# A hybrid decoder block on one Trainium2 core: seven products in the last MLP pass of a group, and the next rows normalised and split one pass earlier

## The reference

```
u = rmsnorm(x) @ w_in                     # 1024 x 3608, split by column
h_m = mLSTM over chunks of 64 (4 heads);  h_g = gated linear attention (4 heads)
x = x + concat(h_m, h_g) @ w_out
x = x + softmax(rmsnorm(x) @ wq_x @ K^T / 16) @ V @ wo_x      # K, V from mem, 4 heads
x = x + square(relu(rmsnorm(x) @ w1)) @ w2                    # 1024 -> 4096 -> 1024
out = rmsnorm(x)
```

## Time and profile before

| | |
|---|---|
| median of three runs | 2837.98 us (2837.52 to 2838.74) |
| the profiled execution | 2838.17 us, its span 2836.6 us |
| instructions | 44515 |
| granted TensorE clock, mean | 0.999 of full speed |
| DMA | 375.50 MB, 132 GB/s on average |
| TensorE / VectorE / ScalarE / GpSimd busy | 99% / 63% / 52% / 33% of the span |

### The profile page before, as it was taken

The page is one execution under the profiler, slowest core; times in us unless marked ns, Lnnn a source line. Parts: engine busy times, 40 slices in busy tenths (PEclk is TensorE's granted clock), DMA queues, the critical chain, the costliest instruction groups (busy, mean ns, idle before and its releaser), DMA issues.

```text
span 2836.6 us, 44515 instructions
## 1 busy us (share of the span) xinstructions
PE 2814.4 (99%) x15148; PEld 2341.6 (83%) x15148; DVE 1778.3 (63%) x2969; ACT 1467.3 (52%) x3006; POOL 924.4 (33%) x1214
## 2 busy tenths in 40 slices
PE   8999999999999999999999999999999999999998
PEld 8888888888888888888888878888888888888887
DVE  6476774666576755556767675466557675545665
ACT  6554444555455444554645544455545544455553
POOL 5264553444135400232326320044322540023430
PEclk9999999999999999999999999999999999999999
DMA  6732575544542222354454222254454223234442
GB/s 218 246 105 68 176 265 176 190 151 133 136 165 82 76 89 90 111 171 142 146 148 146 68 83 90 90 186 147 131 146 164 82 72 92 91 98 147 149 149 82
DMA packets 178823, 375.50 MB, mean 132 GB/s; under 512 B 13808, under 2 KB 13952, under 8 KB 178592
## 3 DMA queue, kind: packets, MB, share of 16 engines
q1 hardware_dynamic: 155216, 300.45, 34.3%
q0 software_dynamic: 20704, 67.33, 7.2%
q10 hardware_dynamic: 2672, 4.76, 0.5%
HBM read 332.60 MB, written 29.39 MB: 128 GB/s over the span
## 4 chain that ended last, share of the span: by engine, by line
PE 95%; DVE 2%; issue 1%; ACT 1%; DMA 0%; DVEq 0%; ACTq 0%
PE bank L1948 47%; PE work L1948 21%; PE bank L2314 14%; PE work L2314 2%; PE work L1962 1%; PE bank L2352 1%; PE work L2063 1%; PE bank L2032 1%; PE work L2101 1%; PE bank L1962 1%; PE work L2123 1%; DVE w_lo L1389 1%; PE work L2010 1%; DVE tok L1575 1%; PE work L2212 1%
## 5 line engine op out<-in xcount | busy, mean ns | idle before, releaser
L872 ACT ACTIVATE w_hi<-raw 128x512 fp32r<-128x512 f32 x1120 | 701.1, 630 | 1034.2 <-PE bank L1948 539.5
L1389 DVE TENSOR_TENSOR w_lo<-raw,w_hi 128x512 fp32r<-128x512 f32 x708 | 515.4, 732 | 837.9 <-ACT w_hi L872 836.5
L1387 DVE SCALAR_TENSOR_TENSOR w_lo<-raw,w_hi 128x512 fp32r<-128x512 f32 x412 | 368.7, 916 | 78.2 <-ACT w_hi L872 77.2
L1948 PE MATMUL bank<-act_hi,w_hi 128*128 128x512 f32 x848 | 333.3, 393 | 0.0
L1948 PE MATMUL bank<-act_lo,w_hi 128*128 128x512 f32 x848 | 330.2, 389 | 0.0
L1948 PE MATMUL bank<-act_hi,w_lo 128*128 128x512 f32 x848 | 330.2, 389 | 0.0
L725 POOL TENSOR_TENSOR hr<-qk 128x256 f32<-128x256 f32 x48 | 35.3, 736 | 784.2 <-ACT qk L1262 784.2
L1948 PE MATMUL bank<-w_hi,act_hi 128*128 128x512 f32 x640 | 255.2, 399 | 0.0
L1948 PE MATMUL bank<-w_lo,act_hi 128*128 128x512 f32 x640 | 249.6, 390 | 0.0
L1948 PE MATMUL bank<-w_hi,act_lo 128*128 128x512 f32 x640 | 249.5, 390 | 0.0
L2314 PE MATMUL bank<-w_hi,h_hi 128*128 128x512 f32 x576 | 224.5, 390 | 0.3
(11 more groups left out here) (391 smaller groups left out, 6075.5 us busy)
## 6 DMA issues: line engine op xcount, KB each, us to landing
raw<-in_w_dram SPq DMA_DIRECT2D x232, 512.0 KB, 3.8
raw<-in_w_in_dram SPq DMA_DIRECT2D x112, 512.0 KB, 3.6
raw<-sums_dram SPq DMA_DIRECT2D x96, 512.0 KB, 3.7
raw<-in_w_out_dram SPq DMA_DIRECT2D x32, 512.0 KB, 3.8
raw<-kq_dram SPq DMA_DIRECT2D x32, 512.0 KB, 3.7
raw<-vo_dram SPq DMA_DIRECT2D x32, 512.0 KB, 3.7
xres<-in_x_dram POOLq DMA_DIRECT2D x16, 512.0 KB, 6.5
early_rows<-in_w_dram POOLq DMA_DIRECT2D x6, 1024.0 KB, 8.9
```

The costliest lines, as they stand in the source:

```text
L872: nc.scalar.activation(w_hi[:, slot, :], raw[:, pair_slot, slot % 2, :], ACT.Copy).then_inc(slab_hi, 1)
L1387: ins = stt(out=w_lo[:, slot, :], in0=src, scalar=1.0, in1=hi, op0=ALU.mult, op1=ALU.subtract)
L1389: ins = tt(w_lo[:, slot, :], src, hi, ALU.subtract)
L1948: ins = mm(dst, left, right, start=(kt == 0 and j == 0), stop=(kt == KT - 1 and j == 2))
```

## The change

The last pass of the first three groups becomes a split pass too; the last group keeps `mlp_pass`. Four more weight sums are made (16 in all): eight through `early_rows`, six through `tok`, of which four wait for the probabilities, and two after `hidden_sums(0)`. The input and output projections get operand buffers of their own, `x_hi` and `x_lo`, which lie over `x_blocks` and `x_turned`; the mixer's smaller buffers now lie over `act_hi` and `act_lo`. The next rows are loaded in pass 1 and their squares, scaling and moves are in pass 2 (`NEXT_PASS`), between GpSimd's differences and S1/S2; the transposes and splits are in the last pass's first half. In the output projection VectorE makes the low parts of tiles 4 and 5 before the split at slab 58 (`FIRST_TURN` - 1). The ring of pairs becomes regular, so its table goes.

```diff
-GROUP_SLABS = MLP_AT[LAST] + 4 * KT
+GROUP_SLABS = MLP_AT[LAST] + PASS_SLABS
-GROUP_PRODS = 2 * PRODUCTS * LAST
+GROUP_PRODS = 2 * PRODUCTS * HB
+PRO_PRODS = 2
+FIRST_TURN = min(TURN_MIX)
-NEXT_SQUARES, NEXT_SCALES, NEXT_TURNS = 0, 5, 20
+NEXT_PASS, NEXT_SQUARES, NEXT_SCALES = HB - 2, 0, 5
+NEXT_TURNS = {1: (0, 1), 2: (2, 3), 3: (4, 5), 4: (6, 7)}
+NEXT_SPLITS = {5: (0, 1), 6: (2, 3), 12: (4, 5), 13: (6, 7)}
-N_SUMS = LAST * HALF
-EARLY_SUMS = 6
+N_SUMS = HB * HALF
+EARLY_SUMS, BEFORE_SUMS = 8, 14
...
+        def free_no(g, hb, q, tile):
+
+            return GROUP_PRODS * g + (PRO_PRODS + 2 * PRODUCTS * hb + 2 * q + tile + 1)
+
+        def sums_done(eng, n):
+
+            eng.wait_ge(sums_stored[n % 4], 16 * (n // 4 + 1))
...
-                def hidden_sums(hb):
+                def hidden_sums(hb, between=None):
...
                         nc.gpsimd.tensor_tensor(diff[:, kt, :], quarter(0, 0, kt), quarter(0, 1, kt),
                                                 ALU.subtract).then_inc(diff_ready, 1)
+                    if between is not None:
+                        between()
                     pool.wait_ge(operand_lo_dve, per_pass(g, N_DVE_LOW, hb, HALF))
...
                     for n in range(EARLY_SUMS):
                         weight_sums(n)
-                        if n in (2, 3):
-                            pool.wait_ge(sums_stored[n - 2], 16)
+                        if 2 <= n < 6:
+                            sums_done(pool, n - 2)
                             load_quarters(n + 2)
                     pool.wait_ge(norm_ss, PRO_ROWS + 16 * g + NCH)
                     load_quarters(EARLY_SUMS)
                     load_quarters(EARLY_SUMS + 1)
-                    for n in range(EARLY_SUMS, N_SUMS):
+                    for n in range(EARLY_SUMS, BEFORE_SUMS):
+                        if n == EARLY_SUMS + 2:
+                            pool.wait_ge(pr_ready, 8 * g + 8)
+                        if n < EARLY_SUMS + 4:
+                            sums_done(pool, n - 4)
                         weight_sums(n)
-                        if n + 2 < N_SUMS:
-                            pool.wait_ge(sums_stored[n], 16)
-                            load_quarters(n + 2)
+                        sums_done(pool, n)
+                        load_quarters(n + 2)
+
+                def next_rows():
+
+                    if first:
+                        for n in (N_SUMS - 2, N_SUMS - 1):
+                            sums_done(pool, n)
+                    if not final:
+                        for i in range(NCH):
+                            pool.dma_start(tok[:, i, :], A["x"][bass.ds((g + 1) * GROUP + i * P, P), :])\
+                                .then_inc(next_in, 16)
+
+                def next_blocks():
+
+                    pool.wait_ge(tok_ready, PRO_ROWS + 8 * g + NCH)
+                    stand_alone(pool)
+                    for n in range(16):
+                        move_blocks(n)
+
                 hidden_sums(0)
...
                 if first:
-                    for n in (N_SUMS - 2, N_SUMS - 1):
-                        pool.wait_ge(sums_stored[n], 16)
...
-                hidden_sums(1)
-                hidden_sums(2)
+                    for n in range(BEFORE_SUMS, N_SUMS):
+                        weight_sums(n)
+                hidden_sums(1, next_rows)
                 if final:
+                    hidden_sums(2)
                     return
-
-                pool.wait_ge(tok_ready, PRO_ROWS + 8 * g + NCH)
-                stand_alone(pool)
-                for n in range(16):
-                    move_blocks(n)
+                hidden_sums(2, next_blocks)
+                hidden_sums(3)
...
+                        if hb == NEXT_PASS and NEXT_SQUARES <= s < NEXT_SQUARES + NCH:
+                            sum_squares(s - NEXT_SQUARES, tok, junk_rows)
+                        for kt in NEXT_SPLITS.get(s, ()) if hb == LAST else ():
+                            act.wait_ge(next_turned, KT * g + KT)
+                            nc.scalar.activation(x_hi[:, kt, :], x_turned[:, kt, :], ACT.Copy,
+                                                 scale=norm_g[:, 0, kt:kt + 1]).then_inc(act_hi_ready, 1)
...
-                for i in range(NCH):
-                    read_out(act, g, GROUP_BANKS - 4 + i)
-                    sum_squares(i)
-                    if i == 1:
+                for q in (Q_P4, Q_P3):
+                    for tile in range(2):
+                        act.wait_ge(prod_free, free_no(g, LAST, q, tile))
+                        sum_squares(2 * ROW_HALF[q] + tile)
+                    if q == Q_P4:
                         split(g, GROUP_SLABS)
...
                 for s in range(B_OUT * KT, B_Q * KT):
+                    if s == FIRST_TURN - 1:
+                        mix_tiles(FIRST_TURN)
                     split(g, s)
...
-                    mix_tiles(s)
+                    if s != FIRST_TURN:
+                        mix_tiles(s)
...
+                        if hb == NEXT_PASS and NEXT_SCALES < s <= NEXT_SCALES + NCH:
+                            scale_row(s - NEXT_SCALES - 1, tok, tok)
+                        for kt in NEXT_TURNS.get(s, ()) if hb == LAST else ():
+                            if kt == 0:
+                                dve.wait_ge(blocks_in, 16 * 16 * (g + 1))
+                            nc.vector.transpose(out=x_turned[:, kt, :].rearrange("p (b n) -> p b n", b=NCH),
+                                                in_=x_blocks[:, :, kt * P:(kt + 1) * P]).then_inc(next_turned, 1)
...
+                    if s == 0:
+                        pe.wait_ge(prod_free, GROUP_PRODS * g + PRO_PRODS)
...
-                for hb in range(LAST):
+                for hb in range(LAST if final else HB):
                     split_pass(hb)
-                mlp_pass()
+                if final:
+                    mlp_pass()
```

More of the change, by code:

```diff
@@ L121, with use_table @@
 N_DVE_LOW, N_POOL_LOW, N_HIGH = HALF * len(DVE_LOW), HALF * len(POOL_LOW), HALF * PRODUCTS
[L124 to L136, removed]
+def use_table(last):
     uses, used, banks, prods = [], 0, 0, 0
-    blocks = [KT] * B_MLP + ([KT] * 2 + [HALF] * PRODUCTS) * LAST + [KT] * 4
+    blocks = [KT] * B_MLP + ([KT] * 2 + [HALF] * PRODUCTS) * LAST + last
     for depth in blocks:
@@ L892, in split @@
                 n = s + LEAD
-                kind, done = USES[n - RING]
+                kind, done = (FINAL_USES if isinstance(g, int) else USES)[n - RING]
                 if kind == "slab":
@@ L1249, in group @@
                         probs_tile(kt)
+                    if r == min(DRAIN_EARLY):
+                        for n in range(EARLY_SUMS):
+                            sums_done(act, n)
                     for kt in DRAIN_EARLY.get(r, ()):
@@ L1396, in split, with tile_lo @@
                 n = s + LEAD
[L1397 to L1399 removed]
+                split_lo(slab_no(g, n), n % RING, n // 2 % PAIRS, scalar)
+            def tile_lo(count, kt, width, gain, hi_lo=(x_hi, x_lo), out_of=wbank):
                 dve.wait_ge(act_hi_ready, count + 1)
@@ L1935, in slab @@
                     if kt == 0 and prior is not None:
-                        pe.wait_ge(bank_free, prior + (i if not turned else (i + 2) % 4) + 1)
+                        pe.wait_ge(bank_free, prior + i + 1)
                     dst = into[i][:, 0:width]
@@ L2045, in block_slab @@
                         pe.wait_ge(act_lo_ready, TRS * g + PRO_TR + tile_count + kt + 1)
-                    slab(slab_no(g, s), kt, major, use_no(g, u - 4) if waits else None, a_hi, a_lo, into=into,
-                         turned=u == 0)
+                    if s == 0:
+                        pe.wait_ge(prod_free, GROUP_PRODS * g + PRO_PRODS)
+                    slab(slab_no(g, s), kt, major, use_no(g, u - 4) if waits else None, a_hi, a_lo, into=into)
                 def levels(c, hds):
```

193 lines of the change are left out of this document (90 added, 103 removed).

## The result

The changed kernel takes 2878.93 us (median of four runs, 2874.43 to 2880.76) against 2838.36 us for the kernel before: ratio 1.0137, 95% interval 1.0125 to 1.0149. It is 40.6 us slower. The forecast was 2833.5 us with a range from 2818 to 2838, so it missed the size and the sign. The profiled execution took 2878.17 us, its span is 2876.6 us (before 2836.6), its mean granted clock 0.993.

What follows compares the result with a forecast made beforehand. TensorE, busy 99% of the span, was taken to bound the kernel. The terms -16.3 - 3.2 + 15.4 - 0.4 = -4.5 us, made on the profiled 2838.17 us, gave 2833.5 us, range 2818 to 2838.

Steps and rivals of the forecast that it cites:

- Term 1: Last pass's second half, first three groups: 168 matmuls for 192, no stall, 16.3 us won.
- Term 2: Output projection: tiles 4 and 5 before slab 61's split remove four 0.8 us waits for act_lo, 3.2 us won.
- Term 3: Next rows' sixteen moves on GpSimd's queue in pass 2, ahead of S1/S2, make P6 late: 15.4 us lost.
- I take the gap as it is: GpSimd's gap before the sixteenth move stays 7.95, 8.60 and 9.51 us when the moves go to pass 2.
- rival (c): Moves compete with the product half's weight loads: gap 12 us instead of 8.6; 2848 us at 10 us a group; chance 0.05.
- The upper bound of 25.4 us: Moves in pass 2: most that is lost if TensorE gets nothing of the 2.7 us slack before P6.
- Rival (d): After each wait P6's 24 matmuls run at 1.2 GHz, +16.3 us in all, 2850 us; chance 0.03.
- Term 4: Four more weight sums in the first group, fourteen before GpSimd's pass 0 work: 0.4 us won, bounds -1.6 to +1.6.
- The last two sums fill idle time: First group: GpSimd's last two weight sums fit before pass 1's differences, with nothing charged.
- Term 5: The rest: turns and splits in the last pass's first half, next group's first slab waiting for all products: 0 us.

Runs made afterwards that it cites:

- mended: Changed kernel with all moves behind pass 2's sums, product-bank signal before the store waits, `SPARE` 168, last two weight sums held until pass 0 is out: 2819.14 us.
- turns_alone: Kernel before, with only VectorE's low parts of tiles 4 and 5 made before the split of slab 61: 2834.59 us, ratio 0.9988.
- mended_64: Same as mended but with `SPARE` = 216, so operands stay 64 bytes off as in the changed kernel: 2835.11 us, ratio 0.9990.
- spare168: Changed kernel with `SPARE` 168 instead of 216, so `h` is again a multiple of 256 bytes from `w`: ratio 1.0060 to the kernel before.
- early_inc: Changed kernel with the first product-bank signal given before VectorE's waits for the folded weights' stores instead of after: 2867.51 us, ratio 1.0107.
- blocks_shifted: Kernel before, with 64 bytes of padding put in front of `x_blocks` alone: 2842.90 us, ratio 1.0019.
- pad_all: Kernel before, with 64 bytes put ahead of `act_hi`, so all operands move up together: ratio 1.0023.
- before_shifted: Kernel before, with `SPARE` 216 instead of 232, so `h`, `pt` and `x_blocks` move by 64 bytes against the weights: ratio 1.0043.
- aligned: Changed kernel with `SPARE` 200 instead of 216, so `h` is 128 bytes off a multiple of 256 from `w`: ratio 1.0180 to the kernel before.
- moves_late: Changed kernel with all sixteen moves behind pass 2's sums, and turns and splits in the last pass's second half: 2846.84 us, ratio 1.0032.
- sixteenth_later: Changed kernel with fifteen moves kept in pass 2 and only the sixteenth issued behind that pass's sums: 2848.16 us, ratio 1.0036.

## Why the prediction was wrong

**Term 1, right.** 168 matmuls for 192 in three groups, with no stall. mended shows the 38.08 us of the sum; the 38.46 of the changed kernel is the address. The 16.3 us are there.

**Term 2, right.** The wait for act_lo is gone in the changed kernel, and turns_alone gives 3.3 us for 3.2.

**Term 3, mis-sized; the first of two steps that failed.** The mechanism was the one forecast, down to the start of the moves (T + 30.2, measured 671.67 - 641.5 = 30.2) and TensorE's stop within P7 for ScalarE and VectorE (all of the wait fell there, none before P6). The failing step is "I take the gap as it is". The gap was 12.9 us and not 8.6. Put into the forecast's own working this gives GpSimd free at T + 55.6 and P6 at 55.6 + 8.15 = T + 63.75; the first low part ends at about 704.85, T + 63.4. The loss is then 9.3 us a group, and 10 were measured, 30 in all for 15.4. So rival (c) is what happened in size, with its threshold of 12 us and its 10 us a group, but not for its reason. I gave it 0.05, because I looked for a reason only in the traffic of weight loads; that could be at most the 1.5 us of the new place, and the larger part was the 64 bytes in `x_blocks`' address. The upper bound of 25.4 us had the same fault: it bounded the slack and held the gap fixed.

**The clock, present but small.** Rival (d) was right that the clock would fall, as the Trainium skill's page "TensorE: Matmul & The Clock Gate", Part 1, has it: 0.50 after the waits of 5.1 and 7.5 us. I held the waits to be too short for it. But it lasted for twelve matmuls of P7 and not through P6's 24. At full clock P7 would have ended near 703.5, and TensorE would have waited for P6's low parts until 704.85; at half clock it was there at 705.89. So the fall costs about 1 us a group net, and 2.4 us at the start of the first group, where nothing hides it.

Two readings behind this were too quick. The prediction says that TensorE was idle for 1.6 us at most; its list of waits also has 7.1 us at the start of the run (`PE work L1981 <- ACT tok L917: 7.1, 1, 7.1`), and the sixteen 128 x 128 matmuls behind that take 3.57 us, where the next eight of that shape, at 10.74, take 1.10. The windows put the clock at 1.00 there all the same, so whether that is the clock stays open. And a wait needn't be long for it: in other runs it fell after 1.8 to 3.0 us (last section).

**Term 4, right for the fourteen sums, wrong for the last two.** GpSimd's fourteenth sum is stored from 483.14 on, and pass 0's first difference is at 495.20, so the sums don't hold it; the wait for pr went from 1.6 to 1.1 us. "The last two sums fill idle time" was wrong: they fill GpSimd's idle time and slow VectorE, 3.0 us.

**Term 5, the second step that failed.** I charged the rest at nothing, and two things were in it. The added signal stands behind VectorE's waits for DMAs, which I had looked at only for later groups, where it costs little (the 1.9 us before the gate matmuls may belong to it; the profile doesn't say). In the first group it cost 7.5 us by the rows. And the operands' addresses, of which I said nothing: 16.0 us by mended against mended_64. The rows give the same order: about 6550 matmuls have `h`, `x` or `pt` moving against the weights, at up to 0.2289 for 0.2267, at most 14 us, and about 1150 of the input projection have `x` stationary, at 0.2333, 8 us more; a bound of 22 us. These 16.0 us and the 8.0 us by which the waits in pass 2 shrank make 24.0, and spare168 gave 23.4.

**The sum with the measured sizes:** -16.3 - 3.3 + 30 + 7.5 + 3.0 + 16.0 = +36.9 us, for 40.0 between the two spans. Of the 3 us that are left, 1.9 are the waits before the gate matmuls; all of it is within what the runs spread. From the other end it closes better: taking all four causes out leaves the first two terms, 2838 - 19.5 = 2818.5, and mended took 2819.1. That it closes to 0.6 us is partly luck: its interval is 2814 to 2822, and it still has the 2.7 us before the gate matmuls. The mend of the last two sums wasn't run by itself. Its 3.0 us are from the row, and part of them may belong to the signal, since early_inc halved that wait.

## What to carry to other kernels

Read a diff for what it does to addresses too. A changed padding, or a buffer that moves, can alter the pace of every matmul that reads it and the time of every DMA that writes it, with no wait to show for it; divide a long row of matmuls by its count in both traces before looking at waits. When a cost is a queue's pause whose reason the trace doesn't show, the bound has to vary the pause, and if one issue of many is the one that pauses, put that one behind the urgent work and leave the others. When a signal is added, look at what its engine waits for just above it.

## What the runs showed of the hardware

The pace of fp32r matmuls of 128 x 512 depends on where the two operands lie to each other in SBUF: 0.2267 us at a distance that is a multiple of 256 bytes, 0.2289 at 64 bytes off, 0.2325 at 128 off (the moving operand `h` against the weights), and 0.2333 at 64 off with `x` stationary and the weights moving. Moving all by 64 bytes leaves 0.2267. Other offsets weren't tried, and no run shows why.

SBUF to SBUF moves with runs of 128 bytes are slower when the written block lies 64 bytes off a multiple of 128 bytes, and GpSimd's pause before the sixteenth issue is longer. Both also depend on where in the schedule the moves stand, so compare within a line. What the pause waits for isn't shown.

| the moves stand | median landing, block on a multiple / 64 off | pause, block on a multiple / 64 off |
|---|---|---|
| in the last pass (before, turns_alone / blocks_shifted, pad_all, before_shifted) | 6.3 to 6.4 / 8.0 to 8.4 us | 8.0 to 9.5 / 12.7 to 13.6 us |
| in pass 2, ahead of the sums (aligned, spare168 / changed kernel, early_inc) | 6.8 / 8.6 to 8.7 us | 9.5 to 10.8 / 12.7 to 13.1 us |
| behind pass 2's sums (mended / mended_64, moves_late) | 8.8 / 9.5 to 10.3 us | 11.3 to 12.0 / 13.6 to 15.6 us |

VectorE's low part of a slab (128 x 512) took 0.69 us with GpSimd idle, up to 1.3 us beside GpSimd's 128 x 256 operations, and up to 2.4 us beside its 128 x 512 weight sums (changed kernel, first group).

The granted clock fell to 0.50 after each wait of over 4 us behind the first rows, for six to thirteen matmuls: after 7.4 to 7.7 us in the changed kernel and early_inc, and after 4.2 to 5.5 us in the changed kernel, aligned, spare168, moves_late and sixteenth_later. After shorter waits it went both ways. After the wait of 3.0 us for `xres` it stayed at 1.00 in the changed kernel and in spare168, and fell for seven matmuls in moves_late and sixteenth_later, where the wait is the same. It also fell after 2.1 us in mended, 2.0 in blocks_shifted and 1.8 in pad_all, and stayed after 2.5 in before_shifted and 2.8 in aligned. So the length of a wait alone doesn't decide it, and a wait of 2 or 3 us can cost some 1.4 us more behind it (an estimate: seven matmuls, 0.2 us each). The fourth matmul behind the wait of 3.0 us starts 0.23 us after the third in the changed kernel and 0.42 in moves_late; TensorE's timelines, in this order:

```profile
561.15 0.39 PE L2377 MATMUL bank<-act_hi,w_lo 128*128 128x512 f32 x1
561.38 0.39 PE L2377 MATMUL bank<-act_hi,w_hi 128*128 128x512 f32 x1
```

```profile
561.35 0.63 PE L2378 MATMUL bank<-act_hi,w_lo 128*128 128x512 f32 x1
561.77 0.63 PE L2378 MATMUL bank<-act_hi,w_hi 128*128 128x512 f32 x1
```
